# Output stage of a hybrid layer on one core: reciprocal roots by logarithm and exponential on ScalarE

## The chip, the cores and the metric

The kernel runs on one core of a Trainium2 chip. The metric is the device time of one launch in microseconds, lower is better. The text calls the engines as the profile does: PE (TensorE), ACT (ScalarE), DVE (VectorE), POOL (GpSimd) and SP (SyncE).

## The reference

One decoder layer over 16 meta tokens and 1024 positions of width 1024. An RMS-normalised input goes through one projection and feeds an HGRN2 recurrence (4 heads of 128) and a gated short convolution (4 groups of 128). Both outputs are normalised per group of 128, concatenated and projected; then comes a mixture of 64 experts (top 8 by sigmoid scores) with one shared expert. The change concerns the two normalisations at the seam:

```
def group_rmsnorm(x, g, n_groups):
    xf = x.reshape(x.shape[:-1] + (n_groups, x.shape[-1] // n_groups))
    y = xf * lax.rsqrt(jnp.mean(xf * xf, axis=-1, keepdims=True) + EPS)
    return y.reshape(x.shape) * g
...
o = group_rmsnorm(o, norm_g, HGRN_HEADS) * jax.nn.silu(g_out)     # HGRN2 half
y_conv = group_rmsnorm(b_gate * conv, norm_g, CONV_GROUPS)        # convolution half
h = h + jnp.concatenate([y_hgrn, y_conv], axis=-1) @ w_out
h = h + moe_ffn(rmsnorm(h, norm_ffn_g), ...)
```

`moe_ffn` scores every row by a sigmoid of its product with the router's weights, takes the eight best experts, and adds a shared expert (SwiGLU of width 256).

## The kernel before

The program has three stages, one after the other, each a block in which five engines run their own instruction streams and meet at semaphores. The first (`phase_front`, to about 438 us) does the input projection, the recurrence and the convolution. The second (`phase_out_route`, about 438 to 699 us) is the output stage, which the change touches. The third (`phase_experts`, from 699 us) runs the experts and the last normalisation.

The output stage works on eight tiles of 128 rows (j = 0 to 7, `TT` = 8). For tile j:

- ACT squares both halves (`squares`, L1299 and L1300) into the scratch tile R (two buffers, by j mod 2; the profile shows it as place).
- PE sums the squares over the 128 channels of each group with a matrix of ones into PSUM (`means`, L1155, tile ms).
- ACT turns the sums into roots (`roots`, L1305, two Sqrt activations: first the gated half, then the convolution half) back into R.
- DVE (`mix`) takes the reciprocal of the convolution half (L1374), multiplies it in (L1376), and tells PE (semaphore s_y); then the reciprocal of the gated half (L1378), the products with the sigmoid gate (L1380, L1382) and with the recurrence's output (L1384), and s_y again.
- PE projects (`project(j, half, part)`, L1169): two column halves, part 0 from the convolution, part 1 from the gated half, into PSUM op.
- DVE adds that to the residual row tile (`residual`, L1391); ACT squares and sums the rows (`row_squares`, L1319) and takes the root of the mean (L1321); DVE takes its reciprocal (L1397) and scales the rows (`normed`, L1402).
- PE transposes them (`turn`, L1182), ACT copies the transposes out of PSUM (`keep`, L1312), PE makes the router's logits (`logits`, L1193), ACT the sigmoid (`score`, L1327), DVE chooses eight experts (`choose`, mask MK at L1416), PE counts ranks (`ranks`, L1201 and L1203), DVE places the rows (`place`, L1426 to L1438), POOL scatters the table entries.
- From j = 3 on the shared expert of an earlier tile joins: `hidden` (PE, L1223), `shared_sigmoid` (ACT, L1333), `shared_hidden` (DVE), `down` (PE, L1236), `accumulate` (DVE, L1454).

The order on each engine is written out by hand. Turn j of the loop:

```
PE:   project(j,0,0)*, project(j,0,1), means(j+2), turn(j-1), project(j,1,0), project(j,1,1), logits(j-1),
      project(j+1,0,0)*, hidden(j-3), ranks(j-1), down(j-4)         * ahead of time for j in SOON = (2, 3)
ACT:  squares(j+2), roots(j+2), keep(j-1), row_squares(j), score(j-1), shared_sigmoid(j-3), gate_sigmoid(j+2)
DVE:  mix(j+1), shared_hidden(j-4), residual(j), normed(j), choose(j-1), place(j-1), accumulate(j-4)
```

`means(j)` waits for the squares of tile j (s_sq) and for the roots of tile j - 1 (s_rt), since both use the PSUM tile ms. The activation tables are not in the code: a pass of the compiler puts an ACT_TABLE_LOAD ahead of an activation whose function is not in the active set.

Of the kernel before, what the change touches and what calls it, by code (L numbers as in the profile page):

```python
# [10 lines left out]
ACT = mybir.ActivationFunctionType  # L11

P = 128
D = 1024
KT = D // P
T = 1024
TT = T // P
META = 16
ALL = META + T
HEADS = 4  # L20
# [956 lines left out]
def phase_out_route(nc, ins, K, xn2_d, acc_d, tbl_d):  # L977
# [4 lines left out]
    with ExitStack() as ctx:  # L982
# [5 lines left out]
        sem = lambda n: ctx.enter_context(nc.semaphore(n))  # L988
# [7 lines left out]
        R = [work[:, i * D:i * D + D].rearrange("p (h t) -> p h t", h=2 * HEADS) for i in range(2)]  # L996
# [6 lines left out]
        bias = tail[:, KT * E_N:(KT + 1) * E_N]  # L1003
        sh = sb("sh", [P, 2 * TT])
# [23 lines left out]
        ms = [ps(f"ms{i}", [P, HEADS, P]) for i in range(2)]  # L1028
# [7 lines left out]
        s_h = [sem(f"h_in{i}") for i in range(NH)]  # L1036
        s_k0, s_k = sem("patterns_cleared"), sem("patterns_set")
        s_sig, s_ag, s_ix = sem("sigmoids"), sem("slots_written"), sem("indices_ready")
        s_sq, s_ms, s_rt = sem("squares"), sem("mean_squares"), sem("roots")
        s_y, s_op, s_h2 = sem("mixed"), sem("out_projected"), sem("residual_added")  # L1040
        s_s2, s_r2, s_x2 = sem("squares_summed2"), sem("root2"), sem("xn2_ready")
        s_t2, s_e2 = sem("xn2_turned"), sem("xn2_kept")
        s_xw = [sem(f"xn2_written{i}") for i in range(2)]
        s_lg, s_sc, s_mk, s_ga, s_rk, s_sl = (sem(n) for n in ("logits", "scores_r", "chosen", "gates_r", "ranks", "ranks_read"))
# [101 lines left out]
        def _(pe):  # L1146
            done = {"turn": 0, "down": 0}

            def means(j):

                pe.wait_ge(s_sq, j + 1)
                if j:
                    pe.wait_ge(s_rt, j)
                for k in range(2):
                    last = pe.matmul(ms[k][:, :, :].rearrange("p h t -> p (h t)"), K.ones[:, :],  # L1155
                                     R[j % 2][:, HEADS * k:HEADS * k + HEADS, :].rearrange("p h t -> p (h t)"), start=True, stop=True)
                last.then_inc(s_ms, 1)
# [136 lines left out]
        @block.scalar  # L1294
        def _(act):
            def squares(j):
                if j >= 2:
                    act.wait_ge(s_y, 2 * j - 2)
                act.activation(R[j % 2][:, 0:HEADS, :], K.QO[:, :, j * P:j * P + P], ACT.Square)  # L1299
                act.activation(R[j % 2][:, HEADS:2 * HEADS, :], YC[:, :, j * P:j * P + P], ACT.Square).then_inc(s_sq, 1)  # L1300

            def roots(j):
                act.wait_ge(s_ms, j + 1)
                for k in range(2):
                    last = act.activation(R[j % 2][:, HEADS * k:HEADS * k + HEADS, :], ms[k][:, :, :], ACT.Sqrt,  # L1305
                                          bias=K.eps[:, 0:1], scale=1.0 / P)
                last.then_inc(s_rt, 1)

            def keep(j):
                act.wait_ge(s_t2, j + 1)  # L1310
                for k in range(2):
                    last = act.copy(K.xT[:, 4 * k:4 * k + 4, j * P:j * P + P], td[k][:, :, :])  # L1312
                last.then_inc(s_e2, 1)

            def row_squares(j):
                if j:
                    act.wait_ge(s_s2, j)
                act.wait_ge(s_h2, 2 * j + 2)
                act.activation(junk, H[j % NH], ACT.Square, accum_out=sh[:, j:j + 1]).then_inc(s_s2, 1)  # L1319
                act.wait_ge(s_s2, j + 1)  # L1320
                act.activation(sh[:, TT + j:TT + j + 1], sh[:, j:j + 1], ACT.Sqrt, bias=K.eps[:, 0:1], scale=1.0 / D).then_inc(s_r2, 1)  # L1321

            def score(j):
                act.wait_ge(s_lg, j + 1)
                if j:
                    act.wait_ge(s_ga, j)
                act.activation(SC[:, :], sm[:, 0:E_N], ACT.Sigmoid).then_inc(s_sc, 1)  # L1327

            def shared_sigmoid(j):
                act.wait_ge(s_gu, j + 1)  # L1330
                if j:
                    act.wait_ge(s_hs, j)
                act.activation(sgs[:, :, :], gu_of(j)[:, 0:2, :], ACT.Sigmoid).then_inc(s_sg, 1)  # L1333

            def gate_sigmoid(j):
                if j >= 2:
                    act.wait_ge(s_y, 2 * j - 2)
                act.activation(sg[j % 2], G[:, :, j * P:j * P + P], ACT.Sigmoid).then_inc(s_sig, 1)

            squares(0)  # L1340
            roots(0)
            gate_sigmoid(0)
            gate_sigmoid(1)
            squares(1)
            roots(1)
            for j in range(TT):
                if j + 2 < TT:
                    squares(j + 2)
                    roots(j + 2)
                if j >= 1:  # L1350
                    keep(j - 1)
                row_squares(j)
                if j >= 1:
                    score(j - 1)
                if j >= LAG:
                    shared_sigmoid(j - LAG)
                if j + 2 < TT:
                    gate_sigmoid(j + 2)
            keep(TT - 1)
            score(TT - 1)  # L1360
            for j in range(TT - LAG, TT):
                shared_sigmoid(j)

        @block.vector
        def _(dve):
            step = Chain(dve, s_d)
            tt, ts, stt = nc.vector.tensor_tensor, nc.vector.tensor_scalar, nc.vector.scalar_tensor_tensor

            def mix(j):

                dve.wait_ge(s_rt, j + 1)
                r, cols = R[j % 2], slice(j * P, j * P + P)
                conv, gated = r[:, HEADS:2 * HEADS, :], r[:, 0:HEADS, :]
                step(nc.vector.reciprocal(conv, conv))  # L1374
                for h in range(HEADS):
                    last = stt(YC[:, h, cols], YC[:, h, cols], K.ng[:, 1, h:h + 1], conv[:, h, :], ALU.mult, ALU.mult)  # L1376
                last.then_inc(s_y, 1)
                step(nc.vector.reciprocal(gated, gated))  # L1378
                dve.wait_ge(s_sig, j + 1)
                step(tt(gated, gated, sg[j % 2], ALU.mult))  # L1380
                for h in range(HEADS):
                    last = stt(G[:, h, cols], G[:, h, cols], K.ng[:, 0, h:h + 1], gated[:, h, :], ALU.mult, ALU.mult)  # L1382
                step(last)
                tt(K.QO[:, :, cols], K.QO[:, :, cols], G[:, :, cols], ALU.mult).then_inc(s_y, 1)  # L1384
# [8 lines left out]
            def normed(j):  # L1393
                if j == 0:
                    dve.wait_ge(s_c, 16)
                dve.wait_ge(s_r2, j + 1)
                step(nc.vector.reciprocal(sh[:, TT + j:TT + j + 1], sh[:, TT + j:TT + j + 1]))  # L1397
                if j >= 2:
                    dve.wait_ge(s_t2, j - 1)
                    dve.wait_ge(s_xw[j % 2], 16 * (j // 2))  # L1400
                by_k = [a.rearrange("p (k t) -> p k t", t=KT) for a in (H[j % NH], gffn[:, :])]
                stt(X2[j % 2].rearrange("p (t k) -> p k t", t=KT), by_k[0], sh[:, TT + j:TT + j + 1], by_k[1], ALU.mult, ALU.mult) \  # L1402
                    .then_inc(s_x2, 1)
# [588 lines left out]
```

## Time and profile before

| | us |
|---|---|
| median of three runs (lowest to highest) | 1634.29 (1633.58 to 1634.79) |
| span of the profiled execution, first to last instruction | 1628.9 |
| median less that span | 5.4 |
| output stage, from the first means to the start of the experts | 439.7 to 698.8 |

The profiled execution has no time of its own beside its span; the 5.4 us are what lies around a span of this kind in the runs. A span is read from the first to the last instruction; busy times of the engines overlap each other, so they are compared with a stretch and not added up. A timeline shows idle time ahead of an instruction only where the engine had nothing to do, with the instruction that released it.

### The profile page before, as it was taken

The numbers are of one execution on the slowest core, as the hardware profiler recorded it, in microseconds if no ns is written. First come the engines' busy times: TensorE is split into PE (matmuls) and PEld (weight loads), VectorE is DVE, ScalarE is ACT, GpSimd is POOL, SyncE is SP. The second block draws the span as 40 slices with busy tenths as digits, with TensorE's granted clock in tenths as the row PEclk, the third lists the DMA queues.
The fourth block names the chain that finished last, engine by engine and source line by source line (L and its number), as shares of the span: only waits on it lengthen the run. The fifth ranks groups of instructions, "written<-read, shape, count | busy, mean of one in ns | idle before, by whom it ended". The sixth has DMA issues, their size and how long they took to land.

```text
span 1628.9 us, 30259 instructions
## 1 busy us (share of the span) xinstructions
PE 1553.9 (95%) x10204; PEld 1337.6 (82%) x10204; DVE 761.0 (47%) x1536; ACT 653.2 (40%) x1054; POOL 671.1 (41%) x825
## 2 busy tenths in 40 slices
PE   6999999999798999899999999999999999999991
PEld 5789989989644667789999999999999999999990
DVE  4333788788688774433333333333333333333333
ACT  6434545444433312034444444444444444444443
POOL 0422245063303222435555554555555555555541
PEclk9999999999999999999999999999999999999996
DMA  5389321211250021479999999999999999999976
GB/s 183 99 290 309 123 78 52 77 55 52 98 216 27 30 62 66 165 267 307 318 318 326 313 305 320 314 314 314 321 308 314 309 315 315 314 313 314 313 234 221
DMA packets 100744, 366.18 MB, mean 225 GB/s; under 512 B 22279, under 2 KB 32424, under 8 KB 79710
## 3 DMA queue, kind: packets, MB, share of 16 engines
q1 hardware_dynamic: 60622, 246.60, 41.9%
q0 software_dynamic: 40080, 119.05, 26.4%
q8 instruction: 23, 0.38, 0.1%
q14 instruction: 19, 0.16, 0.0%
HBM read 300.68 MB, written 73.91 MB: 230 GB/s over the span
## 4 chain that ended last, share of the span: by engine, by line
PE 54%; DMA 1%; issue 0%; ACT 0%; POOL 0%; DVE 0%; SPq 0%; POOLq 0%; ACTq 0%
PE gu L1761 35%; PE ype L1783 4%; PE yrest L1772 4%; PE ype L1784 4%; PE ype L1785 4%; PE xp L1740 3%; PE xp L1747 1%; DMA A<-acc_rows 1%; DMA acc_rows<-YE,sia 1%; POOL acc_rows L1674 0%; DVE A L1947 0%; SPq L1634 0%; ACT junkf L1897 0%; ACT XS L1840 0%; PE ype L1747 0%
## 5 line engine op out<-in xcount | busy, mean ns | idle before, releaser
L1761 PE MATMUL gu<-XS,place 128*128 128x160 f32 x4160 | 586.0, 299 | 0.4 <-ACT XS L1836 0.4
L1761 PEld LDWEIGHTS gu<-XS,place 128*128 128x128 f32 x4160 | 573.5, 190 | 5.7 <-ACT XS L1840 0.7
L1910 DVE TENSOR_TENSOR WL<-place,WH 128x2048 fp32r<-128x2048 f32 x65 | 149.3, 2297 | 315.0 <-ACT WH L1832 315.0
L1674 POOL DMA_INDIRECT acc_rows<-YF,sib x65 | 105.5, 1624 | 197.8 <-issue 155.4
L1845 ACT ACTIVATE SS<-gu 128x160 f32<-128x160 f32 x130 | 39.4, 303 | 362.7 <-PE gu L1761 362.7
L1915 DVE TENSOR_TENSOR SS<-SS,gu 128x160 f32<-128x160 f32 x130 | 41.3, 317 | 253.5 <-ACT SS L1845 253.5
L1660 POOL COPY gta<-tables 128x1 f32 (+1 forms) x65 | 140.6, 2163 | 0.0
L1855 ACT ACTIVATE YE<-ype,gta 128x512 f32<-128x512 f32 x130 | 89.5, 688 | 109.7 <-PE ype L1785 109.7
L1131 POOL DMA_INDIRECT slot_table<-pay,si x64 | 62.0, 968 | 172.4 <-DVEq L1440 159.6
L1832 ACT ACTIVATE WH<-place 128x2048 fp32r<-128x2048 f32 x65 | 123.5, 1900 | 0.7 <-issue 0.7
L1679 POOL DMA_INDIRECT acc_rows<-YE,sia x65 | 103.5, 1593 | 43.9 <-issue 23.5
L1783 PE MATMUL ype<-WH,hidh 128*128 128x512 f32 x260 | 109.2, 420 | 0.0
L1784 PE MATMUL ype<-WL,hidh 128*128 128x512 f32 x260 | 102.6, 395 | 0.0
L1785 PE MATMUL ype<-WH,hidr 128*128 128x512 f32 x260 | 101.3, 390 | 0.0
L1647 POOL DMA_INDIRECT wi<-xn_rows,gi x64 | 65.0, 1015 | 54.9 <-POOL gi L1644 51.6
L1783 PEld LDWEIGHTS ype<-WH,hidh 128*128 128x128 f32 x260 | 48.7, 187 | 35.7 <-issue 26.8
L1836 ACT COPY XS<-xp 128x512 f32<-128x512 f32 x130 | 69.8, 589 | 8.6
L1772 PE MATMUL yrest<-place,HF 128*32 128x256 f32 x1040 | 69.6, 385 | 0.3 <-DVE WL L1910 0.3
L1169 PE MATMUL op<-wo,place 128*128 128x512 f32 x128 | 59.9, 612 | 8.2 <-DVE place L1376 5.9
L1740 PE MATMUL xp<-ident,wi 128*128 128x128 f32 x520 | 67.4, 273 | 0.0
L367 PE MATMUL bank<-xT_high,wf_parts 128*128 128x384 f32 (+2 forms) x192 | 67.2, 350 | 0.0
L368 PE MATMUL bank<-xT_low,wf_parts 128*128 128x384 f32 (+2 forms) x192 | 64.9, 338 | 0.0
(317 smaller groups left out, 2798.2 us busy)
## 6 DMA issues: line engine op xcount, KB each, us to landing
place<-in_w_gate_e SPq DMA_DIRECT2D x65, 1024.0 KB, 7.1
place<-in_w_up_e SPq DMA_DIRECT2D x65, 1024.0 KB, 9.9
place<-in_w_down_e SPq DMA_DIRECT2D x65, 1024.0 KB, 14.0
place<-in_w_in POOLq DMA_DIRECT2D x16, 512.0 KB, 7.0
late_parts<-wq_parts POOLq DMA_DIRECT2D x8, 1024.0 KB, 5.9
late_parts<-xn_parts POOLq DMA_DIRECT2D x8, 1024.0 KB, 6.1
wf_parts<-late_parts POOLq DMA_DIRECT2D x8, 1024.0 KB, 5.1
w_low<-late_parts POOLq DMA_DIRECT2D x8, 1024.0 KB, 5.1
```

What stands on the lines that cost most here:

```text
L1660: last = pool.tensor_copy(gt[q][r][:, :], K.gate[r][:, bass.ds(n, 1)])
L1674: pool.indirect_dma_start(acc_q, bass.IndirectOffsetOnAxis(ap=si[q][1][:, :], axis=0), YF[q][:, :], None, compute_op=ALU.add, bounds_check ...
L1679: pool.indirect_dma_start(acc_d, bass.IndirectOffsetOnAxis(ap=si[q][0][:, :], axis=0), YE[q][:, :], None, compute_op=ALU.add, bounds_check ...
L1740: last = pe.transpose(xp[t // 4][:, t % 4, :], rows[:, t, :], K.ident[:, :])
L1761: last = pe.matmul(gu[f][:, k, :], raw[:, t, f * P:f * P + P], XS[:, q, t, :], start=(t == 0), stop=(t == KT - 1))
L1772: last = pe.matmul(yr[j * CAP1:(j + 1) * CAP1, :], HF[q][:, f, P:CAP], raw[:, f, j * DQ:(j + 1) * DQ], start=(f == 0), stop=(f == 1), tile ...
L1783: pe.matmul(yp[g][:, :], hh, high[:, f, cols], start=(f == 0), stop=False)
L1784: pe.matmul(yp[g][:, :], hh, low[:, f, cols], start=False, stop=False)
L1785: last = pe.matmul(yp[g][:, :], hl, high[:, f, cols], start=False, stop=(f == 1))
L1832: act.activation(WH[q][:, :], WR[q][2][:, :], ACT.Copy).then_inc(s_dhi, 1)
L1855: act.activation(YE[q][:, 512 * g:512 * g + 512], yp[g][:, :], ACT.Copy, scale=gt[q][0][:, 0:1]).then_inc(s_ya, 1)
L1910: tt(WL[q][:, :], WR[q][2][:, :], WH[q][:, :].bitcast(F32), ALU.subtract).then_inc(s_dlo, 1)
```

## The change

In place of a Sqrt on ACT and a reciprocal on DVE, the reciprocal root is made on ACT alone as exp(-0.5 ln(mean + eps)).

- `roots(j)` now does the convolution half first (k = 1), then the gated half (k = 0); each is an Ln from PSUM ms into R (L1306 of the changed file), a wait for it (new semaphore s_ln), and an Exp in place with scale -0.5 (L1308). Each half raises s_rt by one, so s_rt counts two per tile: `means` waits for 2j, `mix` for 2j + 1 ahead of the convolution half and for 2j + 2 ahead of the gated half.
- `mix` loses its two reciprocals of 128 x 512.
- `row_squares(j)` does the same for the 128 x 1 column of row means (L1323 and L1325, new semaphore s_l2), and `normed` loses its reciprocal.

```diff
--- before.py
+++ after.py
@@ -1036,9 +1036,9 @@
         s_h = [sem(f"h_in{i}") for i in range(NH)]
         s_k0, s_k = sem("patterns_cleared"), sem("patterns_set")
         s_sig, s_ag, s_ix = sem("sigmoids"), sem("slots_written"), sem("indices_ready")
-        s_sq, s_ms, s_rt = sem("squares"), sem("mean_squares"), sem("roots")
+        s_sq, s_ms, s_ln, s_rt = sem("squares"), sem("mean_squares"), sem("logs"), sem("roots")
         s_y, s_op, s_h2 = sem("mixed"), sem("out_projected"), sem("residual_added")
-        s_s2, s_r2, s_x2 = sem("squares_summed2"), sem("root2"), sem("xn2_ready")
+        s_s2, s_l2, s_r2, s_x2 = sem("squares_summed2"), sem("log2"), sem("root2"), sem("xn2_ready")
         s_t2, s_e2 = sem("xn2_turned"), sem("xn2_kept")
         s_xw = [sem(f"xn2_written{i}") for i in range(2)]
         s_lg, s_sc, s_mk, s_ga, s_rk, s_sl = (sem(n) for n in ("logits", "scores_r", "chosen", "gates_r", "ranks", "ranks_read"))
@@ -1150,7 +1150,7 @@
 
                 pe.wait_ge(s_sq, j + 1)
                 if j:
-                    pe.wait_ge(s_rt, j)
+                    pe.wait_ge(s_rt, 2 * j)
                 for k in range(2):
                     last = pe.matmul(ms[k][:, :, :].rearrange("p h t -> p (h t)"), K.ones[:, :],
                                      R[j % 2][:, HEADS * k:HEADS * k + HEADS, :].rearrange("p h t -> p (h t)"), start=True, stop=True)
@@ -1301,10 +1301,11 @@
 
             def roots(j):
                 act.wait_ge(s_ms, j + 1)
-                for k in range(2):
-                    last = act.activation(R[j % 2][:, HEADS * k:HEADS * k + HEADS, :], ms[k][:, :, :], ACT.Sqrt,
-                                          bias=K.eps[:, 0:1], scale=1.0 / P)
-                last.then_inc(s_rt, 1)
+                for k in (1, 0):
+                    half = R[j % 2][:, HEADS * k:HEADS * k + HEADS, :]
+                    act.activation(half, ms[k][:, :, :], ACT.Ln, bias=K.eps[:, 0:1], scale=1.0 / P).then_inc(s_ln, 1)
+                    act.wait_ge(s_ln, 2 * j + 2 - k)
+                    act.activation(half, half, ACT.Exp, scale=-0.5).then_inc(s_rt, 1)
 
             def keep(j):
                 act.wait_ge(s_t2, j + 1)
@@ -1318,7 +1319,10 @@
                 act.wait_ge(s_h2, 2 * j + 2)
                 act.activation(junk, H[j % NH], ACT.Square, accum_out=sh[:, j:j + 1]).then_inc(s_s2, 1)
                 act.wait_ge(s_s2, j + 1)
-                act.activation(sh[:, TT + j:TT + j + 1], sh[:, j:j + 1], ACT.Sqrt, bias=K.eps[:, 0:1], scale=1.0 / D).then_inc(s_r2, 1)
+                root = sh[:, TT + j:TT + j + 1]
+                act.activation(root, sh[:, j:j + 1], ACT.Ln, bias=K.eps[:, 0:1], scale=1.0 / D).then_inc(s_l2, 1)
+                act.wait_ge(s_l2, j + 1)
+                act.activation(root, root, ACT.Exp, scale=-0.5).then_inc(s_r2, 1)
 
             def score(j):
                 act.wait_ge(s_lg, j + 1)
@@ -1368,14 +1372,13 @@
 
             def mix(j):
 
-                dve.wait_ge(s_rt, j + 1)
+                dve.wait_ge(s_rt, 2 * j + 1)
                 r, cols = R[j % 2], slice(j * P, j * P + P)
                 conv, gated = r[:, HEADS:2 * HEADS, :], r[:, 0:HEADS, :]
-                step(nc.vector.reciprocal(conv, conv))
                 for h in range(HEADS):
                     last = stt(YC[:, h, cols], YC[:, h, cols], K.ng[:, 1, h:h + 1], conv[:, h, :], ALU.mult, ALU.mult)
                 last.then_inc(s_y, 1)
-                step(nc.vector.reciprocal(gated, gated))
+                dve.wait_ge(s_rt, 2 * j + 2)
                 dve.wait_ge(s_sig, j + 1)
                 step(tt(gated, gated, sg[j % 2], ALU.mult))
                 for h in range(HEADS):
@@ -1394,7 +1397,6 @@
                 if j == 0:
                     dve.wait_ge(s_c, 16)
                 dve.wait_ge(s_r2, j + 1)
-                step(nc.vector.reciprocal(sh[:, TT + j:TT + j + 1], sh[:, TT + j:TT + j + 1]))
                 if j >= 2:
                     dve.wait_ge(s_t2, j - 1)
                     dve.wait_ge(s_xw[j % 2], 16 * (j // 2))
```

The order of the instructions on ACT as compiled, with the table loads that the compiler's pass places. Around `roots` of a tile (tile 4 and its like; place is the scratch tile R, ms the sums, eps the constant), before:

```order
-L1338 ACTIVATE place<-G 128x512
-L1299 ACTIVATE place<-QO 128x512
-L1300 ACTIVATE place<-place 128x512
-L1305 ACT_TABLE_LOAD
-L1305 ACTIVATE place<-ms,eps 128x512 x2
-L1312 COPY xT<-td 128x4x128 x2
```

and with the change, where L1306 is the Ln, L1308 the Exp, L1313 the copies of `keep`:

```order
+L1342 ACTIVATE place<-G 128x512
+L1299 ACTIVATE place<-QO 128x512
+L1300 ACTIVATE place<-place 128x512
+L1306 ACT_TABLE_LOAD
+L1306 ACTIVATE place<-ms,eps 128x512
+L1308 ACT_TABLE_LOAD
+L1308 ACTIVATE place<-place 128x512
+L1306 ACT_TABLE_LOAD
+L1306 ACTIVATE place<-ms,eps 128x512
+L1308 ACT_TABLE_LOAD
+L1308 ACTIVATE place<-place 128x512
+L1313 COPY xT<-td 128x4x128 x2
```

One load ahead of two Sqrt became four loads, one ahead of each Ln and of each Exp.

The second place is `row_squares` and `score` of a tile (sh holds the row sums and roots, SC the scores), before:

```order
-L1312 COPY xT<-td 128x4x128 x2
-L1319 ACTIVATE place,sh<-wi 128x1024
-L1321 ACTIVATE sh<-sh,eps 128x1
-L1327 ACT_TABLE_LOAD
-L1327 ACTIVATE SC<-sm 128x64
-L1333 ACTIVATE sgs<-gub 128x256
```

and with the change, where L1323 is the Ln, L1325 the Exp, L1331 the scores' sigmoid:

```order
+L1313 COPY xT<-td 128x4x128 x2
+L1320 ACTIVATE place,sh<-wi 128x1024
+L1323 ACT_TABLE_LOAD
+L1323 ACTIVATE sh<-sh,eps 128x1
+L1325 ACT_TABLE_LOAD
+L1325 ACTIVATE sh<-sh 128x1
+L1331 ACT_TABLE_LOAD
+L1331 ACTIVATE SC<-sm 128x64
+L1337 ACTIVATE sgs<-gub 128x256
```

One load (for the sigmoid) became three. Over the stage the loads go from 18 to 57. The order of PE's instructions doesn't change, and DVE's rows differ only by the three reciprocals of each tile that are gone.

## Rows read from the trace of the kernel before

**Rows 1.** The page: the span, and part 1, busy time of each engine.
```profile
span 1628.9 us, 30259 instructions
...
PE 1553.9 (95%) x10204; PEld 1337.6 (82%) x10204; DVE 761.0 (47%) x1536; ACT 653.2 (40%) x1054; POOL 671.1 (41%) x825
```

**Rows 2.** Stretches: from:to and length, busy us of PE PEld DVE ACT POOL, PEclk, DMA, GB/s.
```profile
480.00:520.00 40.00, 35.71 (x118) 18.23 (x117) 30.99 (x90) 14.16 (x23) 10.23 (x11) 1.00 0.07 27
...
520.00:600.00 80.00, 80.00 (x392) 52.40 (x391) 61.16 (x147) 22.88 (x39) 25.43 (x27) 1.00 0.11 37
...
438.00:700.00 262.00, 241.96 (x1107) 151.72 (x1108) 172.65 (x441) 70.95 (x116) 67.89 (x79) 0.98 0.28 104
```

**Rows 3.** Timeline of PE: start, us, line, operation, tiles, count, [idle before it <- releaser].
```profile
439.74 3.64 PE L1155 MATMUL ms<-place,ones 128*128 128x512 f32 x4 [2.87 <-ACT place L1300]
...
449.30 5.69 PE L1169 MATMUL op<-wo,place 128*128 128x512 f32 x8 [5.92 <-DVE place L1376]
...
469.28 3.67 PE L1169 MATMUL op<-wo,place 128*128 128x512 f32 x8 [0.55 <-DVE SW L1391]
...
492.00 0.41 PE L1201 MATMUL sm<-MK,before 128*128 128x64 f32 x2 [0.94 <-DVEq L1417]
...
495.73 1.88 PE L1155 MATMUL ms<-place,ones 128*128 128x512 f32 x4
...
505.19 1.90 PE L1193 MATMUL sm<-place,xT 128*128 128x64 f32 x16
...
508.83 3.67 PE L1169 MATMUL op<-wo,place 128*128 128x512 f32 x8 [1.75 <-DVE wi L1391]
...
514.10 0.43 PE L1201 MATMUL sm<-MK,before 128*128 128x64 f32 x2 [1.60 <-DVEq L1417]
...
529.28 7.36 PE L1223 MATMUL gub<-xT,SW 128*128 128x128 f32 x64
...
536.48 0.37 PE L1201 MATMUL sm<-MK,before 128*128 128x64 f32 x2
```

**Rows 4.** The timeline of ACT, one tile of the stage.
```profile
497.65 1.27 ACT L1305 ACTIVATE place<-ms,eps 128x512 f32<-128x512 f32 x2 [5.12 <-PE ms L1155]
...
498.81 1.07 ACT L1312 COPY xT<-td 128x512 f32<-128x512 f32 x2
...
509.38 1.06 ACT L1319 ACTIVATE place<-wi 128x1024 f32<-128x1024 f32 x1 [9.51 <-DVE wi L1391]
...
510.57 0.29 ACT L1321 ACTIVATE sh<-sh,eps 128x1 f32<-128x1 f32 x1
...
510.88 1.28 ACT L1327 ACT_TABLE_LOAD   x1
...
512.17 0.23 ACT L1327 ACTIVATE SC<-sm 128x64 f32<-128x64 f32 x1
...
512.81 0.62 ACT L1299 ACTIVATE place<-QO 128x512 f32<-128x512 f32 x1
```

**Rows 5.** The timeline of ACT in the stage ahead: an Exp of the same shape.
```profile
413.87 0.63 ACT L704 ACTIVATE wi<-wi 128x512 f32<-128x512 f32 x1
```

**Rows 6.** The timeline of DVE, start and the same tile.
```profile
448.10 1.14 DVE L1376 SCALAR_TENSOR_TENSOR place<-place,ng 128x128 f32<-128x128 f32 x4
...
485.88 0.69 DVE L1391 TENSOR_TENSOR H<-H,op 128x512 f32<-128x512 f32 x1 [1.48 <-PE op L1169]
...
497.67 3.35 DVE L1374 RECIPROCAL place<-place 128x512 f32<-128x512 f32 x1
...
510.89 0.16 DVE L1397 RECIPROCAL sh<-sh 128x1 f32<-128x1 f32 x1 [1.61 <-ACT sh L1321]
...
511.09 2.00 DVE L1402 SCALAR_TENSOR_TENSOR place<-wi,sh,SW 128x1024 f32<-128x1024 f32 x1
```

**Rows 7.** The view of stretches: the clock before and after the idle time ahead of 439.74.
```profile
438.00:439.00 1.00, 0.00 (x0) 0.00 (x0) 0.12 (x1) 0.46 (x1) 0.47 (x5) 1.00 0.00 0
...
440.00:443.00 3.00, 3.00 (x4) 0.92 (x4) 0.00 (x0) 0.99 (x1) 0.24 (x1) 0.50 0.97 362
```

## The prediction

> **What bounds the kernel now.** I read the page first: PE is busy for 1553.9 of 1628.9 us, DVE for less than half of that [rows 1]. That is an average over three stages, so the second view is that of stretches, where the reader should see PE at 241.96 of 262 us in the output stage, and at 80.00 of 80 between 520 and 600 us [rows 2]. So from tile 3 on nothing but PE's own work counts, and an edit to DVE or ACT gains nothing there; it can only lose, by making PE wait. The third view, PE's timeline [rows 3], shows where PE does wait in the tiles before: 5.92 us for the first product of DVE, then 0.55, 0.94, 1.75 and 1.60 us, all released by DVE. The last four are 4.8 us, the most that a faster DVE can give besides the first wait.
>
> **What goes.** Per tile two reciprocals of 3.35 us and one of 0.16 us [rows 6], over eight tiles 8 x 6.86 = 54.9 us of DVE's time.
>
> **What comes.** On ACT, per tile two Exp of 128 x 512 at 0.63 us (an Exp of that shape [rows 5]) and one of a column at 0.29 us (as the column's root [rows 4]); the two Ln replace the two Sqrt, which took 1.27 us together, 0.68 each [rows 4]. The order of ACT shows the real cost: 39 more table loads, at 1.28 us each 50 us of ACT's time. A load starts when the activation before it has ended and holds the next one: from the end of the column's root (510.57 + 0.29) to the sigmoid at 512.17 are 1.31 us [rows 4]. The waits on the new semaphores s_ln and s_l2 cost nothing, because a load lies between each Ln and its Exp and is longer than the Ln takes to land; without that cover I would put them at 0.1 us each.
>
> [...]
>
> **One tile on ACT, from the moment t = 0 when the sums of `means` are there** (497.65 in the rows). Roots: 0.68 + 1.31 + 0.63 per half, and 1.31 between the halves: the convolution half is ready at 2.6, the gated half at 6.55 (both roots were ready at 1.27 before). The copies of `keep` take 1.07 and end at 7.5; PE comes to `logits` at 505.19 - 497.65 = 7.54 [rows 3, 4], so it waits 0.1 at most. Before, `keep` had 5 us of slack: that is what covered ACT. Then the projection's last result comes at 7.7, DVE no longer stands in its reciprocals and adds it by 8.4 (0.69 [rows 6]), the row squares take 1.19, then load, Ln, load, Exp 3.2: the row factor is there at 12.8. Before, the squares began at 509.38, t = 11.7, and the root was there at 13.2. Load, scores, gate sigmoid (1.31 + 0.64 [rows 4]) bring ACT to 14.8, and the next squares (0.62 and 0.52) end at 15.9. `normed` starts at 12.8, and PE's `ranks` follows 514.10 - 511.09 = 3.0 later [rows 3, 6], at 15.9; before it came at 16.45. So in the steady state the 6.86 us taken off DVE and the slower ACT cancel. From tile 3 on PE reaches `ranks` at t = 16.5, after 7.36 us of `hidden` [rows 3], so the 15.9 are covered, by 0.6 us. In tiles 6 and 7 there are no roots, one more load than before, and `hidden` as cover: nothing.
>
> **Where it doesn't cancel** is the start, where ACT works with nothing ahead:
> - First product. The sums are there at 443.4; the convolution half at 446.05, its multiplication (1.14 [rows 6]) at 447.2: PE starts 2.0 us earlier than at 449.30. But it ran there at the low clock: 8 matmuls took 5.69 us against 3.67 later [rows 3], 2.0 lost, so some 4 us at half speed, to 453.3. From 447.2 that would be 6.1 us at half speed and 3.0 lost: 1.0 of the gain comes back.
> - `means(2)`: the squares of tile 2 stand behind the 6.55 us of the roots of tile 1, and end at 463.35, when PE has been free for 1.0. So far nothing gained.
> - The wait of 0.55 goes, since `residual(0)` is no longer late: -0.55.
> - `means(3)`: sums of tile 2 at 465.3, roots to 471.8, row squares of tile 0 to 473.0, load, Ln, load, Exp to 476.2, load and gate sigmoid to 478.0, squares of tile 3 to 479.2. PE is there at 475.4: **+3.8**.
> - `ranks(0)`: 16.2 after the sums of tile 3 (15.9, and 0.3 for the two small steps of DVE's first `choose`); PE, without `hidden`, is there at 12.9 (`logits` at 7.54, 1.9, a projection of 3.5). It waits 3.3 where it waited 0.94: **+2.4**.
> - Tile 2: the wait of 1.75 goes, that of 1.60 becomes 3.1: -0.25.
> - Four `logits` at 0.1: +0.4.
>
> Sum: -0.55 + 3.8 + 2.4 - 0.25 + 0.4 = 5.8; the roundings hold some 0.4, and I take **+5.6**.
>
> **The clock.** [...] Through waits of up to 1.75 us it stayed at 1.00 [rows 2, 3]. The three new waits of 3.8, 3.3 and 3.1 us are all longer than the one that cost it. Bounds: none falls, 0; each falls, 6. They are nearest to the row of 2.87, yet that row followed on light work, so I take one fall, **+2.0**.
>
> The profiled execution has a span of 1628.9, 5.4 under the median; the span should become 1636.5 and the median 1634.3 + 7.6 = **1641.9 us**.
>
> **Rivals.**
> - The clock holds: 1639.9. For it: PE is full on both sides of each new wait, which it was not at 439.74. It is part of the range.
> - ACT's chain is longer than the rows make it (a wait ahead of each Exp, an Ln slower than Sqrt). Seven loads and seven activations lie in the loop of 15.9 us, and behind 16.5 the cover in tiles 3 to 5 is gone too. At 0.15 us more for each of the seven pairs, 1.05 a tile: 3 us in the three paced tiles, 0.4 in each of three covered ones, 4.5 with `logits`: 1646.5, more if two clocks fall.
> - Faster: Ln and Exp run from one table. Then the roots take 2.6, the row chain has one load, all new waits on ACT vanish, and DVE's relief stays: the waits of 0.55 and 1.75 go, 1.60 shrinks to 0.5, the start gives some 0.6: -4.1, 1630.2. It decides as soon as the loop on ACT ends before PE needs it at t = 12.9 without loads inside the pairs. Against it: the order of the changed kernel has a load ahead of each Ln and each Exp. [...]
> - No change: PE's waits move but sum to about what they were, because the losses at `means(3)` and `ranks(0)` are smaller (a load begins while ACT waits). Against it: in both, ACT is busy without a gap. 1634 to 1637.5.
>
> **How the numbers follow.** Forecast with at least one fall of the clock 0.50; clock holds 0.27; longer chain 0.09; no change 0.10; one table 0.04. Low end 1637.0 leaves out most of the last two, high end 1648.0 takes in two or three falls and most of the longer chain. A measurement of this kernel can tell some 0.2%, 3.3 us. Faster 0.04, same 0.10, slower 0.86.
>
> **What would show it.** 57 loads in the stage instead of 18; `means(3)` waiting some 4 us for ACT's squares, `ranks(0)` and `ranks(1)` some 3 us; no wait of PE for `residual`; PE full from the first `hidden` on; DVE's busy time down 55 us, ACT's up some 60; experts starting 7 to 8 us later, and of unchanged length. I am wrong if PE waits in tiles 3 to 5 by more than 0.2 us, if a load costs less between an Ln and its Exp, or if the clock is at 1.00 throughout.

## The result, and the profile after

The change made the kernel slower: 1640.72 us (median of four runs, 1639.95 to 1642.25) against 1634.08 (four runs, 1633.58 to 1634.79), a ratio of 1.005 with a 95% interval of 1.0038 to 1.0061. The medians lie 6.6 us apart; 7.6 were forecast.

The page of the changed kernel, its span and busy times, against [rows 1]:

```profile
span 1639.6 us, 30298 instructions
...
PE 1560.4 (95%) x10204; PEld 1339.4 (82%) x10204; DVE 706.5 (43%) x1512; ACT 715.9 (44%) x1117; POOL 672.6 (41%) x825
```

The span grew by 10.7 us, more than the 6.6 of the medians; the experiments come back to that. DVE lost 54.5 us of busy time and ACT gained 62.7. The groups of ACT over the output stage (line, operation, count, busy us, mean ns, idle before) show what ACT gained: 48 loads at 1283 ns in the four groups of Ln and Exp (9 more stand at L1331 and L1342, 57 in all), and the 16 Exp:

```profile
L1306 ACT ACT_TABLE_LOAD x16 | 20.5, 1283 | 0.3
L1308 ACT ACT_TABLE_LOAD x16 | 20.5, 1283 | 0.3
...
L1323 ACT ACT_TABLE_LOAD x8 | 10.3, 1283 | 0.1
L1325 ACT ACT_TABLE_LOAD x8 | 10.3, 1283 | 0.1
L1308 ACT ACTIVATE place<-place 128x512 f32<-128x512 f32 x16 | 10.1, 629 | 0.2
```

The timeline of PE, the rows that answer to [rows 3]:

```profile
440.22 3.56 PE L1155 MATMUL ms<-place,ones 128*128 128x512 f32 x4 [2.87 <-ACT place L1300]
447.67 5.20 PE L1169 MATMUL op<-wo,place 128*128 128x512 f32 x8 [3.89 <-DVE place L1379]
453.94 1.98 PE L1155 MATMUL ms<-place,ones 128*128 128x512 f32 x4 [1.07 <-ACT place L1300]
...
479.41 3.78 PE L1155 MATMUL ms<-place,ones 128*128 128x512 f32 x4 [3.50 <-ACT place L1300]
...
500.52 0.41 PE L1201 MATMUL sm<-MK,before 128*128 128x64 f32 x2 [3.50 <-DVEq L1419]
500.76 5.35 PE L1169 MATMUL op<-wo,QO 128*128 128x512 f32 x8
...
523.68 0.43 PE L1201 MATMUL sm<-MK,before 128*128 128x64 f32 x2 [2.75 <-DVEq L1419]
...
685.28 5.37 PE L1236 MATMUL td<-SW,hs 128*128 128x512 f32 x8 [1.96 <-DVE wi L1456]
...
708.64 0.63 PE L1749 MATMUL ype<-ident,wi 128*128 128x128 f32 x4 [1.72 <-PEq L982]
```

PE no longer waits for DVE's residual (no row of that kind is left up to 648 us). In its place stand 3.50 us ahead of `means(3)`, released by ACT's squares, and 3.50 and 2.75 us ahead of `ranks(0)` and `ranks(1)`. In two places the work behind the wait is slow as well: `means(3)` takes 3.78 us in place of 1.88, and the projection at 500.76 takes 5.35 in place of 3.65. The rows of stretches, in the form of [rows 2], show the granted clock there; it is the third column from the right, 1.00 for the full clock, and 0.57 where most of a stretch was granted 0.50:

```profile
477.00:484.00 7.00, 4.59 (x9) 2.42 (x10) 5.44 (x12) 4.38 (x7) 0.00 (x0) 0.57 0.18 75
485.00:500.00 15.00, 12.03 (x40) 5.97 (x38) 3.56 (x8) 12.96 (x19) 0.00 (x0) 1.00 0.02 7
501.50:504.50 3.00, 3.00 (x5) 1.20 (x4) 2.05 (x13) 0.00 (x0) 1.03 (x1) 0.57 0.01 3
```

What ACT does ahead of `means(3)`, from its timeline, is the chain of the prediction, without a gap. The row squares of tile 0 end at 473.25, and then come

```profile
473.27 1.28 ACT L1323 ACT_TABLE_LOAD   x1
474.56 0.29 ACT L1323 ACTIVATE sh<-sh,eps 128x1 f32<-128x1 f32 x1
474.88 1.28 ACT L1325 ACT_TABLE_LOAD   x1
476.17 0.20 ACT L1325 ACTIVATE sh<-sh 128x1 f32<-128x1 f32 x1
476.39 1.28 ACT L1342 ACT_TABLE_LOAD   x1
477.69 0.63 ACT L1342 ACTIVATE place<-G 128x512 f32<-128x512 f32 x1
...
478.74 0.61 ACT L1300 ACTIVATE place<-place 128x512 f32<-128x512 f32 x1
```

A load costs 1.3 us between an Ln and its Exp too (474.56 + 0.29 to 476.17). From the first `means` to the first product of the experts the stage took 268.4 us (440.22 to 708.64), where it took 259.1 (439.74 to 698.81). Of the 10.7 us by which the span grew, 9.3 lie in this stage, 0.5 ahead of it and 0.9 behind it.

### The profile page after: what moved, and what is told of

It is laid out like the page before. It is cut to its first block, busy times and chain, and to the rows that moved or that the text cites. A ratio compares the mean times of both kernels' runs of the same rounds, so it can differ in the third digit from the quotient of the medians.

```text
span 1639.6 us, 30298 instructions
## 1 busy us (share of the span) xinstructions
PE 1560.4 (95%) x10204; PEld 1339.4 (82%) x10204; DVE 706.5 (43%) x1512; ACT 715.9 (44%) x1117; POOL 672.6 (41%) x825
## 4 chain that ended last, share of the span: by engine, by line
PE 54%; DMA 1%; issue 0%; ACT 0%; POOL 0%; DVE 0%; SPq 0%; POOLq 0%; ACTq 0%
PE gu L1763 34%; PE ype L1785 4%; PE yrest L1774 4%; PE ype L1786 4%; PE ype L1787 3%; PE xp L1742 3%; PE xp L1749 1%; DMA A<-acc_rows 1%; DMA acc_rows<-YE,sia 1%; POOL acc_rows L1676 0%; DVE A L1949 0%; SPq L1636 0%; ACT junkf L1899 0%; ACT XS L1842 0%; PE ype L1749 0%
## 5 line engine op out<-in xcount | busy, mean ns | idle before, releaser
L1649 POOL DMA_INDIRECT wi<-xn_rows,gi x64 | 65.0, 1015 | 54.9 <-POOL gi L1646 51.6
L367 PE MATMUL bank<-xT_high,wf_parts 128*128 128x384 f32 (+2 forms) x192 | 67.2, 350 | 0.0
L369 PE MATMUL bank<-xT_high,wf_parts 128*128 128x384 f32 (+2 forms) x192 | 64.6, 337 | 0.0
```

## The experiments

The theories, as the expectations name them. **A**: the 39 added table loads lengthen ACT's chain and make PE wait. **B**: the chain is long by its added activations and waits, with or without loads. **C**: a good part of the loss is the clock that falls behind the new waits. The kernels were timed in three groups, each beside the kernel before on one chip; the medians of before were 1633.28 us (the first four kernels below), 1632.85 (the second execution of before and of the change, both Ln first, one function) and 1633.29 (with filler at the start, and both faster versions again). A ratio is to before in the same group, with its 95% interval behind it.

### The same change with one table for Ln and Exp

A table set that holds both functions is loaded by hand, where the compiler's pass had put a load ahead of each Ln and of each Exp. That leaves 18 loads in the stage. The arithmetic is unchanged.

```diff
+            def both_tables():
+                nc.scalar.add_instruction(mybir.InstLoadActFuncSet(
+                    name=nc.get_next_instruction_name(), act_func_set_id=6, ins=[], outs=[]))
             def roots(j):
+                if j != 2:
+                    both_tables()
                 act.wait_ge(s_ms, j + 1)
...
             def row_squares(j):
...
+                if j >= 6:
+                    both_tables()
                 root = sh[:, TT + j:TT + j + 1]
```

> The change as it is, but a table that holds both functions (set 6) is loaded by hand ahead of each tile's roots and of the row root of tiles 6 and 7, so that no load stands between an Ln and its Exp: 18 loads in the stage, as before the change, instead of 57. Theory A (the 39 added loads are the loss): the roots of a tile take 2.6 us instead of 6.55, PE's waits for means(2), means(3), ranks(0) and ranks(1) shrink to 0, 0, 0.8 and 0.5 us, and the relief of DVE is left: 4 us faster than before the change, 1630 us. Theory B (the longer chain of activations and waits on ACT is the loss, with or without loads): still slower than before by 2 us or more, waits of over 2 us at means(3) and ranks(0).

Measured: 1624.77 us, a ratio to before of 0.995 (0.9936 to 0.9964); again in the last group 1625.17, 0.9951 (0.9937 to 0.9964). Here is ACT in the roots of tile 4 and the row root of tile 2, then PE's timeline:

```profile
494.84 0.69 ACT L1312 ACTIVATE place<-ms,eps 128x512 f32<-128x512 f32 x1 [4.92 <-PE ms L1155]
...
496.80 0.63 ACT L1314 ACTIVATE place<-place 128x512 f32<-128x512 f32 x1
...
504.55 0.30 ACT L1331 ACTIVATE sh<-sh,eps 128x1 f32<-128x1 f32 x1
504.88 0.20 ACT L1333 ACTIVATE sh<-sh 128x1 f32<-128x1 f32 x1
505.10 1.28 ACT L1339 ACT_TABLE_LOAD   x1
```

```profile
447.57 5.37 PE L1169 MATMUL op<-wo,place 128*128 128x512 f32 x8 [3.31 <-DMA wo<-in_w_out]
...
489.19 0.41 PE L1201 MATMUL sm<-MK,before 128*128 128x64 f32 x2 [0.97 <-DVEq L1427]
...
508.15 0.43 PE L1201 MATMUL sm<-MK,before 128*128 128x64 f32 x2 [0.38 <-DVEq L1427]
```

That set 6 holds both functions is shown by this run. These are the groups of ACT in the stage that belong to the roots:

```profile
L1304 ACT ACT_TABLE_LOAD x9 | 11.5, 1283 | 0.2
L1312 ACT ACTIVATE place<-ms,eps 128x512 f32<-128x512 f32 x16 | 10.8, 678 | 36.6 <-PE ms L1155 36.6
L1314 ACT ACTIVATE place<-place 128x512 f32<-128x512 f32 x16 | 10.1, 629 | 0.5
```

The nine loads by hand (L1304) are all that serve them: the 16 Ln and 16 Exp of the roots, and with them the 8 Ln and 8 Exp of the rows (L1331 and L1333), have no load of their own, where each of the 48 had one in the change. The other nine loads stand at the scores' sigmoid (L1339, 7) and at the gate's (L1350, 2).

The roots take 2.6 us (494.84 to 497.43) and the row root 0.5, no load stands inside either, and of PE's waits 0.97 and 0.38 are left, as A had it. B is out: all added activations and semaphores are still there, and some 16 us lie between this kernel and the change. The gain of 8.5 us is twice the 4 that A put on it. The stage shows why: 251.9 us (440.83 to 692.69) against 259.1, 7.2 less. From the start of the first `means` to that of the second PE took 11.9 us (440.83 to 452.77) against 15.1, so the start gave 3.2 where 0.6 was forecast; the rest gave 4.0 where 3.5 was. The first projection was expected to give part of its earlier start back to the low clock, and it gave nothing back (5.37 us, where it had taken 5.69). At 447.57 it now waits for the load of the output weights, which nothing showed before because DVE was later. The stage is 7.2 us shorter than in the execution of before that the prediction read, and 9.3 shorter than in a second one (below); the 8.5 of the medians lie between.

### The two parts alone

Roots only: `row_squares` and `normed` as before. Rows only: `roots` and `mix` as before.

```diff
 roots only, against the change:
-                act.activation(root, sh[:, j:j + 1], ACT.Ln, ...).then_inc(s_l2, 1)
-                act.wait_ge(s_l2, j + 1)
-                act.activation(root, root, ACT.Exp, scale=-0.5).then_inc(s_r2, 1)
+                act.activation(root, sh[:, j:j + 1], ACT.Sqrt, bias=K.eps[:, 0:1], scale=1.0 / D).then_inc(s_r2, 1)
...
+                step(nc.vector.reciprocal(root, root))
 rows only: the same lines the other way, against the kernel before
```

> Only the group roots by Ln and Exp; the row root as before (Sqrt on ACT, reciprocal on DVE). Theory A: one load less in the row chain per tile (2 instead of 3), which ends 1.5 us earlier; waits of 1.0 at means(2), 2.2 at means(3), 2.0 at ranks(0), 1.7 at ranks(1): 1.2 us over before, and up to 2 more if the clock falls: 1635 to 1637. Rival (the four loads of the roots are most of the loss, since they are two thirds of the added loads): 1638 or more, nearly the whole loss.

> Only the row root by Ln and Exp; group roots as before (two Sqrt, two reciprocals of 3.35 us on DVE). Theory A: the row chain gets 2.7 us longer and DVE gives nothing back, so PE waits 1.1 at means(3), 3.6 at ranks(0), 2.0 for the residual of tile 2, 4.5 at ranks(1) and 2.8 at ranks(2): 9.4 us over before without the clock, some 2 to 4 more with it: 1643 to 1648, slower than the whole change. Rival (the parts add up, the row part is the small one with 16 of the 39 loads): 1636 to 1638.

Measured: roots only 1633.06 us, ratio 1.0004 (0.9995 to 1.0013), under the 1635 to 1637 expected; rows only 1641.89 us, ratio 1.0056 (1.0043 to 1.007), under the 1643 to 1648 expected. PE's waits, roots only and then rows only:

```profile
477.53 1.99 PE L1155 MATMUL ms<-place,ones 128*128 128x512 f32 x4 [1.99 <-ACT place L1300]
...
494.69 0.41 PE L1201 MATMUL sm<-MK,before 128*128 128x64 f32 x2 [2.00 <-DVEq L1417]
...
514.87 0.43 PE L1201 MATMUL sm<-MK,before 128*128 128x64 f32 x2 [1.46 <-DVEq L1417]
```

```profile
477.77 1.98 PE L1155 MATMUL ms<-place,ones 128*128 128x512 f32 x4 [0.68 <-ACT place L1300]
...
496.29 0.66 PE L1201 MATMUL sm<-MK,before 128*128 128x64 f32 x2 [3.57 <-DVEq L1419]
496.74 6.42 PE L1169 MATMUL op<-wo,QO 128*128 128x512 f32 x8
...
521.34 0.43 PE L1201 MATMUL sm<-MK,before 128*128 128x64 f32 x2 [3.50 <-DVEq L1419]
...
521.83 5.35 PE L1169 MATMUL op<-wo,QO 128*128 128x512 f32 x8
...
546.17 0.43 PE L1201 MATMUL sm<-MK,before 128*128 128x64 f32 x2 [0.60 <-DVEq L1419]
```

Roots only costs nothing that can be told from zero, though it holds 32 of the stage's 48 loads for Ln and Exp. Its waits of 1.99, 2.00 and 1.46 are close to the 2.2, 2.0 and 1.7 expected, and what DVE no longer does pays for them. The clock held behind all three (`means(3)` took 1.99 us, the projections behind `ranks` 3.65), so nothing came of the up to 2 us that the expectation had added for it. The 32 loads are not free for all that: with two of the four in each tile's roots gone, the change gets 4 to 5 us faster (both Ln first, below).

Rows only, with 16 of the loads, is as slow as the whole change. Its row chain is longer by two loads and an Exp, and DVE gives back only the 0.16 us of the column. PE waits 3.57 at `ranks(0)` (3.6 expected), 3.50 at `ranks(1)` (4.5 expected), 0.68 at `means(3)` (1.1 expected) and 0.60 at `ranks(2)`, in the first covered tile (2.8 expected); the 2.0 expected for the residual of tile 2 are not there. So A had these waits at 9.4 us over before, and they make 4.1. About as much again is the clock: the projections behind the two long waits took 6.42 and 5.35 us in place of 3.65, 4.7 with the 0.25 of `ranks(0)` itself. The rival of that expectation, 1636 to 1638, is out.

By their ratios the two parts alone make 0.7 and 9.1 us, 9.8 together against 7 to 8 for the whole. That would fit a row part that uses up the relief the roots part brings; but the intervals of the ratios are as wide as the difference, so it is not shown.

### The whole change with PE kept busy in its waits

```diff
+            def filler(n, out):
+                for _ in range(n):
+                    pe.matmul(out, K.ones[:, :], K.ident[:, :], start=True, stop=True)
             def means(j):
+                if j == 3:
+                    pe.wait_ge(s_rt, 2 * j)
+                    filler(14, ms[0][:, 0, :])
                 pe.wait_ge(s_sq, j + 1)
...
             def ranks(j):
+                if j < 2:
+                    filler(12, td[0][:, 0, :])
                 pe.wait_ge(s_mk, j + 1)
```

> The whole change, with matmuls into spare PSUM ahead of PE's three new waits (14 ahead of means(3), 12 each ahead of ranks(0) and ranks(1)), so that PE is not idle there; their result is overwritten or not used. Theory C (the clock falls after these waits and costs 4.4 us of the profiled 9.4 in the stage): the granted clock stays at 1.00 from 460 us to the end of the stage, 2 to 4 us faster than the change, 1637 to 1639. Rival (the clock costs nothing that the waits behind it don't absorb): within 1 us of the change, 1640 to 1641.

Measured: 1636.97 us, ratio 1.0024 (1.0015 to 1.0033). The change itself was at 1.005 (1.0038 to 1.0061) and, timed again in the next group, at 1.0046 (1.0032 to 1.006). So the filler gives back some 3.5 us, though its results are not used; with the kernels in different groups, the timings give that size only to within some 2.5 us. PE in the filled waits:

```profile
475.90 3.29 PE L1152 MATMUL ms<-ident,ones 128*128 128x128 f32 x28
479.57 1.98 PE L1163 MATMUL ms<-place,ones 128*128 128x512 f32 x4 [0.38 <-ACT place L1310]
...
497.98 0.43 PE L1211 MATMUL sm<-MK,before 128*128 128x64 f32 x2 [0.58 <-DVEq L1429]
```

`means(3)` is back at 1.98 us, and `ranks(0)` comes 57.9 us after the first `means` (440.07 there) where it came 60.3 after it in the change (500.52 less 440.22). The stage is 4.0 us shorter in all (264.5 for 268.4), with ACT's chain as it was, and the granted clock was 1.00 from 475 to 504 us. So C holds, beside A: 1637 to 1639 had been expected, and of the 6.6 us over before about half goes when the clock doesn't fall behind the new waits.

### Both kernels again, unchanged

> The kernel before, unchanged, for a second profiled execution. Medians put the change 6.6 us over before, the two profiled executions put it 10.7 over (spans 1639.6 and 1628.9). Theory A (the profiled execution of before was a short one, 3 to 4 us under its kind, by clock falls that it happened not to have): a span of 1631 to 1633, with one or two falls more of the clock in the output stage, ratio 1.000. Rival (the span of before is right, and the change has 4 us in its profiled execution that its runs don't have): a span of 1628 to 1629.5.

> The changed kernel, unchanged, beside the others on the same chip: 6 to 7 us over before, span 1637 to 1640. Theory A and C (waits set by ACT, and falls of the clock behind them): the waits at means(3), ranks(0), ranks(1) are again 3.5, 3.5 and 2.8 us within 0.4, and the falls of the clock may lie elsewhere.

Measured: the kernel before 1633.36 us, ratio to itself 1.0002 (0.9993 to 1.0011), with a span of 1632.1; the change, run again, 1640.48, ratio 1.0046 (1.0032 to 1.006), span 1639.8. The profiled execution of before that all terms were taken from was a short one: 1628.9, against 1632.1 here. This is where PE was slower in the second one, rows of the same instructions as in [rows 3] and of the tail:

```profile
509.53 5.30 PE L1169 MATMUL op<-wo,place 128*128 128x512 f32 x8 [1.75 <-DVE wi L1391]
514.81 0.44 PE L1201 MATMUL sm<-MK,before 128*128 128x64 f32 x2
...
655.53 9.04 PE L1223 MATMUL gub<-xT,SW 128*128 128x128 f32 x64 [1.00 <-DVE hs L1448]
...
686.81 0.49 PE L1282 MATMUL op<-ident,wo 118*128 118x118 f32 x2 [1.29 <-DMA wo<-slot_table,rowi]
```

Behind the same wait of 1.75 us the projection here took 5.30 us in place of 3.67, and `hidden` behind a wait of 1.00 took 9.04, where it took 7.41 behind one of 1.01. Over the first 3.5 us of the projection and the first 4 us of `hidden` the granted clock was 0.53 and 0.58 here, and 1.00 there. The same program, with the same waits, loses its clock in one execution and keeps it in another. The first of these falls cost nothing: the wait of 1.60 at `ranks(1)` is gone in exchange. The second cost 1.6. Another 0.4 is no clock but a DMA that PE waited for longer, 1.29 us in place of 0.87. The stage took 261.2 us here (440.33 to 701.53), 2.1 more than in the execution I read, and the span lies 1.3 us under its median where the first lay 5.2 under. So this one is nearer to the usual.

The change's waits in its second execution were 3.50, 3.28 and 2.74 us, against 3.50, 3.50 and 2.75, and its stage 268.8 us. This time the clock fell behind all three:

```profile
522.12 0.43 PE L1201 MATMUL sm<-MK,before 128*128 128x64 f32 x2 [2.74 <-DVEq L1419]
...
522.61 5.35 PE L1169 MATMUL op<-wo,QO 128*128 128x512 f32 x8
```

The same projection took 3.65 us in the first execution, behind a wait of 2.75. `means(3)` took 3.42 and the projection behind `ranks(0)` 5.24. The falls cost 5.0 us together, 4.5 in the first.

### Both Ln first, then both Exp

```diff
-                for k in (1, 0):
-                    half = R[j % 2][:, HEADS * k:HEADS * k + HEADS, :]
-                    act.activation(half, ms[k][:, :, :], ACT.Ln, ...).then_inc(s_ln, 1)
-                    act.wait_ge(s_ln, 2 * j + 2 - k)
-                    act.activation(half, half, ACT.Exp, scale=-0.5).then_inc(s_rt, 1)
+                for k in (1, 0):
+                    act.activation(R[j % 2][:, HEADS * k:HEADS * k + HEADS, :], ms[k][:, :, :], ACT.Ln, ...).then_inc(s_ln, 1)
+                for k in (1, 0):
+                    half = R[j % 2][:, HEADS * k:HEADS * k + HEADS, :]
+                    act.wait_ge(s_ln, 2 * j + 2 - k)
+                    act.activation(half, half, ACT.Exp, scale=-0.5).then_inc(s_rt, 1)
```

> The change with both Ln of a tile first and then both Exp: two loads in the roots instead of four, same arithmetic. Theory A (each load on ACT's chain is 1.3 us): roots of 3.8 us instead of 6.55, waits of 0 at means(2), 1.5 at means(3), 3.4 at ranks(0), 3.1 at ranks(1), which stay because the three loads of the row chain stay; 3.4 us under the change, 1637. Rival (loads in the roots don't matter, they lie beside other work): within 1 us of the change, 1640.

Measured: 1635.40 us, ratio 1.0019 (1.001 to 1.0028), 4 to 5 us under the change in its second timing, where 3.4 were expected:

```profile
476.32 1.98 PE L1155 MATMUL ms<-place,ones 128*128 128x512 f32 x4 [1.20 <-ACT place L1300]
...
494.76 0.66 PE L1201 MATMUL sm<-MK,before 128*128 128x64 f32 x2 [3.49 <-DVEq L1421]
...
517.81 0.44 PE L1201 MATMUL sm<-MK,before 128*128 128x64 f32 x2 [2.88 <-DVEq L1421]
```

The wait at `means(3)` falls from 3.50 to 1.20; those at `ranks` stay at 3.49 and 2.88, because the row chain keeps its three loads. That is A's pattern, place by place. What it gains beyond that fits the clock, which did not fall behind the shorter wait: `means(3)` takes 1.98 us, in the change 3.78 and 3.42. Behind the two waits at `ranks` it fell here too, and the projections took 5.04 and 5.35 us.

### One function in place of two, and filler at the start

```diff
                 for k in (1, 0):
+                    act.activation(R[j % 2][:, HEADS * k:HEADS * k + HEADS, :], ms[k][:, :, :], ACT.Abs_reciprocal_sqrt,
+                                   bias=K.eps[:, 0:1], scale=1.0 / P).then_inc(s_rt, 1)
...
+                act.activation(sh[:, TT + j:TT + j + 1], sh[:, j:j + 1], ACT.Abs_reciprocal_sqrt, bias=K.eps[:, 0:1], scale=1.0 / D).then_inc(s_r2, 1)
```

 Theory A: 1.2 us under the version with one table for Ln and Exp (roots 1.3 us instead of 2.6; waits of 0.6 at ranks(0) and 0.3 at ranks(1)): 9 to 10 us under before, 1623.5 to 1624.5. Rival (what is left of PE's waits is DVE's and the clock's, so a shorter ACT gives nothing more): as the version with one table, 1624.8 within 0.5.

> The one-function version again, as the partner of the two others: 1623.5 to 1625.5, 0 to 1.3 us under the one-table version, since in the profiled executions PE's waits at ranks(0) and ranks(1) were 0.74 and under 0.3 us against 0.97 and 0.38.

> The one-table version again, beside the one-function version on the same chip: 8 us under before, 1624.8. Theory A (PE's waits that ACT sets are gone in both but for 0.4 us): 0 to 1.3 us over the one-function version.

> The one-function version with matmuls into spare PSUM where PE still waits: 5 ahead of means(0), 10 ahead of the first project, 7 ahead of down(5); their results are overwritten. Theory C (what the start still loses is the half clock, which lay over 6.8 of the 14 us from 439.9 to 453.3 and cost 3.4 us, and one fall at 668 us): the granted clock stays at 1.00 after 443 us or falls later, 1.5 to 4 us under the one-function version, 1621 to 1623.5. Rival (the start is bound by the load of the output weights, which PE waited for at 446.5, and by the squares; the clock there hides in those waits): within 1 us of it.

Measured: one function 1625.16 us, 0.9956 (0.9942 to 0.9969), and in the last group 1624.62, 0.9948 (0.9934 to 0.9961); one table beside it 1625.17; with filler 1624.70, 0.9946 (0.9932 to 0.9959). The 1.2 us that A gave to the shorter function can't be told from nothing in these runs. PE's first projection without filler, then PE with it:

```profile
446.49 5.37 PE L1169 MATMUL op<-wo,place 128*128 128x512 f32 x8 [2.99 <-DMA wo<-in_w_out]
```

```profile
439.81 1.97 PE L1162 MATMUL ms<-place,ones 128*128 128x512 f32 x4
441.61 2.39 PE L1152 MATMUL td<-ident,ones 128*128 128x128 f32 x20
446.37 5.37 PE L1178 MATMUL op<-wo,place 128*128 128x512 f32 x8 [2.36 <-DMA wo<-in_w_out]
```

The filler did what it should to `means(0)`, 1.97 us in place of 3.6, and it gained nothing: the first projection starts when the output weights are there, at 446.4 with it and at 446.5 without, and takes 5.37 us in both. So the rival of that expectation was right. The third filler only moved a fall of the clock: `down(5)` took 3.67 us behind it, where it took 5.37 without, but then PE waited 1.44 for a DMA and the 32 matmuls of `hidden` at 678.03 took 5.42, where they took 3.79.

## Why the prediction was right

Point by point, by its own steps; places of the changed profile are given less the 0.5 us by which its stage began later (440.22 for 439.74).

- **The total**: 1641.9 forecast, 1640.72 measured. The waits were read rightly; that the sum came so near is partly luck, since two errors of 3 to 4 us cancel: the span came out 3.1 higher than forecast, mainly by the clock, and what was added to it for the median was some 4 too much.
- **First product**: forecast at 447.2, found at 447.2. It was to lose 3.0 us to the low clock and lost 1.5 (5.20 for 3.67). The gain went into a wait of 1.07 at `means(1)` that was not in my list, and one of 0.83 at `means(2)` (1.0 forecast). Up to there I had 0; it was -0.3.
- **The wait of 0.55** went, as forecast.
- **`means(3)`**: 3.8 forecast, 3.50 found. **`ranks(0)`**: 3.3 and 3.50, so +2.6 for +2.4. **Tile 2**: 3.1 and 2.75, so -0.6 for -0.25. **`logits`**: 0.1 each forecast; no wait stands in the rows, but in tiles 3 to 5 PE came through 0.15 later each (from 533.69 to 539.00 in 5.3 us, before in 5.2), 0.45 in all. These and the start, less 0.2 of a shorter wait at `hidden` in the tail, make 4.9 us where I had 5.6.
- **Tiles 3 to 5**: no wait of PE, as forecast. The tail has the waits it had (0.82 at 658, 1.96 at 685).
- **Busy times**: DVE -54.9 forecast and -54.5 found; ACT some +60 and +62.7.
- **Experts**: forecast to start 7 to 8 us later, with their length unchanged. They started 9.8 later than in the execution I read (708.64 for 698.81), 7.1 later than in its second one, and took 0.9 and 0.4 us longer.
- **The load's price**: 1.3 us, between Ln and Exp as elsewhere: 1283 ns in each of the four groups of loads above, and the next activation starts 0.01 us after the load's end (473.27 + 1.28 to 474.56).
- **The waits on the new semaphores**: behind a load they cost nothing, as forecast (Exp 0.01 us after the load, 474.88 + 1.28 to 476.17). Without that cover 0.1 us was my estimate; in the kernel with one table an Exp starts 0.72 us after its Ln (494.84 to 495.56), where of two Sqrt without such a wait, 0.68 us each and 1.27 together [rows 4], the second starts 0.59 after the first: 0.13.
- **The clock**: seen as a term, but put too low, and on wrong ground. The falls I had to go by were those of the start: a granted clock of 0.50 behind the wait of 2.87 us [rows 7], with 3.64 us for 1.88, 1.8 lost, and the first projection behind the wait of 5.92, 5.69 for 3.67, 2.0 lost [rows 3]. I wrote that through waits of up to 1.75 us it stayed at 1.00, and took one fall for +2.0. In the change it fell behind two of the three new waits, for 4.5 us together: 1.9 at `means(3)`, 0.9 at the transposes behind it and 1.7 at 500.76; in its second execution it fell behind all three, for 5.0. (A further fall, at 685.28, cost nothing: there before waits for a DMA that now comes in time, and 685.28 to 708.64 is as long as 675.49 to 698.81.) Before itself falls behind waits of 1.75 and 1.00 in its second execution and loses 1.6 us by the latter. Against the execution that I read the stage grew by 4.9 + 4.5, the 9.3 us found. Against the second one it grew by 7.2, since 1.6 of clock and some 0.5 of a DMA wait and the start fall to before.
- **From span to median**: I added the stage's growth to a span of 1628.9 and took the 5.4 us up to the median for what lies around every span. The runs show that it isn't: a run of 1641.11 us had a span of 1639.6, one of before with 1633.66 a span of 1632.1, 1.5 us less. The execution of before that I counted from was some 4 us shorter than its kind. So the changed span was forecast at 1636.5 and is 1639.6, 3.1 more, while the median came out 1.2 less than forecast.
- **The rival with one table** had the right mechanism and half of its size: -4.1, where the kernel with one table loaded by hand measured -8.1 to -8.5. Its start gained 3.2 and not 0.6, and behind its waits from 453 to 669 us the clock held, where before lost 1.6 us in one of two executions. Its chance of 0.04 was about whether this kernel would be compiled so, and it was not, with 57 loads in the trace. One set does serve both functions once it is loaded by hand: 24 Ln and 24 Exp behind nine loads, at 1624.8 us; in what was compiled here it is not chosen.

What stays open: why the clock falls in one execution and holds in another behind the same wait, and so whether it would cost the kernels with one table anything. Also not tried is how much of their gain comes from the reciprocals that DVE no longer does, and how much from the convolution half being made and passed on first.

## What to carry to other kernels

Read the compiled order of an engine before costing an edit of its functions: two functions that a set holds in common may still each get a load, at 1.3 us on the chain, and loading the common set by hand turned a loss of 7 us into a gain of 8. Ask which chain a part lies on and what it takes off another engine, not how many instructions it adds: 32 loads in the roots came out even with the reciprocals that went, and 16 in the row chain, with next to nothing taken off, cost 9 us, half of them by the clock. Where waits of 1 to 3 us stand in front of TensorE (1.00, 1.75 and 2.7 here), one profiled execution is not the kernel: read at least two before taking a term of 2 us from it.

## What the runs showed of the hardware

- The granted clock fell behind waits of 1.75 and 1.00 us in one execution of the kernel before and behind neither in another (5.30 against 3.67 us, 9.04 against 7.41), and behind a wait of 2.7 us in one execution of the change and not in the other (5.35 against 3.65), with the work on both sides unchanged.
- Matmuls whose result nobody uses, put into PE's waits, made the change some 3.5 us faster. At the start of the stage the same trick made `means(0)` 1.6 us shorter and the kernel no faster.
